# Expert weights by one 2 MB transfer per matrix, and row transposes with a step of eight

## What is computed

```python
# t: 512 tokens x 1024; each token goes to 2 of 32 experts, with a weight
def block_mlp(args):
    xb, e = args
    return (jax.nn.silu(xb @ w_gate[e]) * (xb @ w_up[e])) @ w_down[e]
# w_gate, w_up: [32, 1024, 512]; w_down: [32, 512, 1024]; all float32
```

## Time and profile before

| | |
|---|---|
| median of three runs | 2282.76 us |
| profiled execution | 2282.8 us, its span 2280.9 us |
| busy: TensorE, VectorE, ScalarE, GpSimd | 96%, 65%, 55%, 13% of the span |
| read from DRAM | 362.9 MB |
| transfers of expert weights | 192 of 1024 KB |
| mean granted TensorE clock | 0.985 |

### The profile page before, as it was taken

The page is one execution under the profiler, slowest core; times in us unless marked ns, Lnnn a source line. Parts: engine busy times, 40 slices in busy tenths (PEclk is TensorE's granted clock), DMA queues, the critical chain, the costliest instruction groups (busy, mean ns, idle before and its releaser), DMA issues. The chain is left out here.

```text
span 2280.9 us, 31925 instructions
## 1 busy us (share of the span) xinstructions
PE 2191.4 (96%) x12430; PEld 1735.7 (76%) x12430; DVE 1480.9 (65%) x1872; ACT 1250.7 (55%) x1695; POOL 300.8 (13%) x342
## 2 busy tenths in 40 slices
PE   7999999999999999899999999999995999999997
PEld 6878658877768787898888888888684777777774
DVE  3533862558888678665324573453447999988897
ACT  4324552478884454652315423244434888888885
POOL 2000001023320122640000000000011111122220
PEclk9999999999999999999999999999996999999999
DMA  6122117422224433011232213333136999999996
GB/s 239 56 74 93 37 38 247 138 75 93 93 83 157 149 112 149 22 40 56 81 104 93 93 47 121 111 122 137 56 141 245 401 405 410 403 406 399 401 398 241
DMA packets 121731, 385.61 MB, mean 169 GB/s; under 512 B 9548, under 2 KB 38532, under 8 KB 96400
## 3 DMA queue, kind: packets, MB, share of 16 engines
q1 hardware_dynamic: 106688, 333.54, 39.3%
q0 software_dynamic: 14416, 44.12, 5.7%
q10 hardware_dynamic: 512, 6.34, 0.7%
HBM read 362.89 MB, written 28.89 MB: 172 GB/s over the span
## 5 line engine op out<-in xcount | busy, mean ns | idle before, releaser
L2387 DVE TENSOR_TENSOR w_lo<-raw,w_hi 128x2048 fp32r<-128x2048 f32 x117 | 268.8, 2298 | 458.2 <-ACT w_hi L1730 458.0
L1730 ACT ACTIVATE w_hi<-raw 128x2048 fp32r<-128x2048 f32 x117 | 223.8, 1913 | 404.6 <-PE bank L900 367.3
L900 PE MATMUL bank<-hT_hi,w_hi 128*128 128x512 f32 x512 | 200.7, 392 | 4.6 <-DVE hT_lo L2451 2.3
L900 PE MATMUL bank<-hT_lo,w_hi 128*128 128x512 f32 x512 | 200.0, 391 | 0.0
L900 PE MATMUL bank<-hT_hi,w_lo 128*128 128x512 f32 x512 | 199.9, 391 | 0.0
L1111 PE MATMUL bank<-hT_hi,w_hi 128*128 128x512 f32 x432 | 173.8, 402 | 0.9 <-DVE hT_lo L2451 0.9
L1111 PE MATMUL bank<-hT_hi,w_lo 128*128 128x512 f32 x432 | 168.2, 389 | 0.0
L1111 PE MATMUL bank<-hT_lo,w_hi 128*128 128x512 f32 x432 | 168.1, 389 | 0.0
L3238 DVE TENSOR_TENSOR e_lo<-eraw,e_hi 128x2048 fp32r<-128x2048 f32 x62 | 141.8, 2288 | 35.6 <-ACT e_hi L2272 34.8
L3122 DVE TENSOR_TENSOR e_lo<-raw,e_hi 128x2048 fp32r<-128x2048 f32 x64 | 146.5, 2289 | 8.8 <-ACT e_hi L2255 8.5
L3122 DVE TENSOR_TENSOR w_lo<-raw,w_hi 128x2048 fp32r<-128x2048 f32 x64 | 144.3, 2285 | 5.8 <-ACT w_hi L2255 5.5
(11 more groups left out here) (608 smaller groups left out, 5202.3 us busy)
## 6 DMA issues: line engine op xcount, KB each, us to landing
raw<-expert_w_gate SPq DMA_DIRECT2D x64, 1024.0 KB
raw<-expert_w_up SPq DMA_DIRECT2D x64, 1024.0 KB
eraw<-expert_w_down SPq DMA_DIRECT2D x64, 1024.0 KB
raw<-w_in SPq DMA_DIRECT2D x40, 1024.0 KB
raw<-even_w_in SPq DMA_DIRECT2D x18, 1024.0 KB
raw<-odd_w_in SPq DMA_DIRECT2D x16, 1024.0 KB
raw<-even_w_out SPq DMA_DIRECT2D x8, 1024.0 KB
raw<-odd_w_out SPq DMA_DIRECT2D x8, 1024.0 KB
```

The source lines that it names most:

```text
L900: mm = pe.matmul(out, st, mv, start=first and x == 0, stop=last and x == 2)
L1730: act.activation(split_to(m)[0][:], raw[n % RAW][:], ACT.Copy).then_inc(sem("hi_done"), 1)
L2387: dve.tensor_tensor(split_to(m)[1][:], raw[split_of[m] % RAW][:], f32(split_to(m)[0][:]), ALU.subtract).then_inc(sem("lo_done"), 1)
```

## The change

The four raw buffers become one tensor `raws`, of which `raw[s]` are views at the same places. A matrix is fetched whole, into `whole[j]` (gate, up, down), by one DMA of 2 MB: partition p gets rows 8p to 8p+7 of gate or up (16 KB side by side in DRAM and in the partition), or rows 4p to 4p+3 of down as before, now both unit halves at once. Everything behind the transfer still works by units of 1 MB, as views of `whole`. The refetch of gate waits for units 0 and 1 of the expert before, that of up for units 2 and 3, that of down for both of its units. The readers of both units of a matrix wait for its one transfer. Since a partition now holds rows 8p to 8p+7, `rows_T` takes every eighth column of `xg`.

```diff
-    raw = [place(f"raw{s}", [P, 4, 512]) for s in range(RAW)]
+    raws = place("raws", [P, 4 * RAW, 512])
+    raw = [raws[:, 4 * s:4 * s + 4] for s in range(RAW)]
...
-    eraw = [raw[(len(units) + k) % RAW] for k in range(4)] + [view(f"eraw{k}", 2, [P, 4, 512], at=8192 * k) for k in range(2)]
+    assert len(units) % RAW in (0, 2)
+    whole = [raws[:, 4 * s:4 * s + KD] for s in ((len(units) + k) % RAW for k in (0, 2))] + [view("eraw_dn", 2, [P, KD, 512])[:]]
+    eraw = [w[:, 4 * u:4 * u + 4] for w in whole for u in range(2)]
...
-        def expert(e, k):
-
-            if k < 4:
-                w = io["expert_w_gate_2" if k < 2 else "expert_w_up_2"][0]
-                return w[bass.ds(e, 1)].rearrange("a (h p k) n -> p (a h) k n", p=P, k=4)[:, k % 2]
-            w = io["expert_w_down_2"][0]
-            return w[bass.ds(e, 1)].rearrange("a (p k) (h n) -> p (a k h) n", p=P, h=2)[:, 4 * (k - 4):4 * (k - 4) + 4]
-
-        def fetch(b, e, ks, first=False, d_done=0):
-            for k in ks:
+        def expert(e, j):
+
+            w = io[("expert_w_gate_2", "expert_w_up_2", "expert_w_down_2")[j]][0][bass.ds(e, 1)]
+            if j < 2:
+                return w.rearrange("a (p k) n -> p (a k) n", p=P)
+            return w.rearrange("a (p k) (h n) -> p (a k h) n", p=P, h=2)
+
+        def fetch(b, e, js, first=False, d_done=0):
+            for j in js:
                 if not first:
-                    if k < 4:
-                        sp.wait_ge(sem("gu_lo"), 4 * b + (k - 3))
+                    if j < 2:
+                        sp.wait_ge(sem("gu_lo"), 4 * b + (2 * j - 2))
                     else:
-                        sp.wait_ge(sem("d_lo"), 2 * b + (k - 5 - d_done))
-                sp.dma_start(eraw[k][:], expert(e, k)).then_inc(sem(f"e_in{k}"), 16)
-
-        GU, DN = range(4), (4, 5)
-        for k in GU:
-            u = units[len(units) - RAW + k]
-            sp.wait_ge(sem("lo_done"), u["split"] + 1)
-            fetch(0, 0, [k], True)
+                        sp.wait_ge(sem("d_lo"), 2 * b - d_done if d_done else 2 * b)
+                sp.dma_start(whole[j][:], expert(e, j)).then_inc(sem(f"e_in{2 * j}"), 16)
+
+        GU, DN = (0, 1), (2,)
+        for j in GU:
+            for u in units[len(units) - RAW + 2 * j:len(units) - RAW + 2 * j + 2]:
+                sp.wait_ge(sem("lo_done"), u["split"] + 1)
+            fetch(0, 0, [j], True)
...
             for f in range(KD):
-                rows = xg[:, 512 * (f // 4) + f % 4:512 * (f // 4) + 512:4]
+                rows = xg[:, f:D:KD]
...
-                pe.wait_ge(*after(f"e_in{4 + u}", 16 * NE))
+                pe.wait_ge(*after("e_in4", 16 * NE))
...
-                act.wait_ge(*after(f"e_in{u}", 16 * b + 16))
+                act.wait_ge(*after(f"e_in{2 * (u // 2)}", 16 * b + 16))
...
-            act.wait_ge(*after(f"e_in{4 + u}", 16 * b + 16))
+            act.wait_ge(*after("e_in4", 16 * b + 16))
```

More of the change, by code:

```diff
@@ L1703, in _ @@
                 rows_there(b)
-                pe.matmul(psum[2][:, 0:BLK], xg[:, 0:512:4], ident[0:BLK, 0:BLK], start=True, stop=True)
+                pe.matmul(psum[2][:, 0:BLK], xg[:, 0:D:KD], ident[0:BLK, 0:BLK], start=True, stop=True)
                 rows_T(b)
```

## The result

The changed kernel takes **2316.95 us** (median; 2315.3 to 2320.43), the kernel before 2282.3 on the same chip: ratio 1.0153, 95% interval 1.0141 to 1.0165. Forecast were 2287 us and a range of 2276 to 2302: wrong by 30 us, on the slower side. The profiled execution took 2315.3 us, 32.5 more than the one before.

A forecast was written before the change was run, and what follows sets the result against it. The prediction took TensorE's pace to bound the loop's first half and the DMA stream's bytes the second. From 2282.8 us, -7.0 + 4.0 + 2.8 + 2.6 + 2.0 = +4.4 gave 2287 us, range 2276 to 2302.

The forecast's parts named there:

- part 3: Expert loop: three whole buffers leave little room before refetch but no stall; 0.1 us per expert, +2.8 us.
- Part 1: Expert loop's weight transfers: half as many packets, 16 KB instead of 8, gain 0.24 us per expert, -7.0 us.
- Part 2: Start of the loop: refetches wait for both halves, +3.0 us, and the first gather is delayed, +1.0; sum +4.0.
- Rival (b): Weight transfers in the loop: the long packets gain nothing, so no -7.0; 2294 us, chance 0.16.
- Part 4: Tail: down of expert 30 lands whole and later, +2.6 us; y_dram reads come behind down of 31, +2.0.
- Part 5: Row transposes on TensorE: loading xg with a step of eight instead of four costs 0 (bound 0.6 us per expert).
- (d): Row transposes on TensorE: step of eight costs as much again as step of four; 2297 or 2312 us, chance 0.10.
- (a): Expert loop: the queue runs dry as down's refetch comes late, 0.5 us or more per expert; 2298 us, chance 0.20.

The follow-up runs named there:

- Late release and late landing: Kernel before, 1 MB transfers kept; a matrix's halves are refetched only when both are split, and readers wait for both halves: 2315.89 us, ratio 1.0139.
- The series above: Changed kernel (2316.95 us), then inside its loop VectorE's split of each second unit halved (2300.17 us), then ScalarE's halved too (2298.73 us); timing only.
- the late release alone: Kernel before, with both halves of a buffer fetched again only when both are split; readers still wait by halves: 2288.48 us, ratio 1.0019.
- two reorderings: Changed kernel with both units of down split before the product: 2338.02 us; changed kernel with y copies ahead of down's first split: 2317.53 us.

## Why the prediction was wrong

**The sum against the traces.** Up to expert 2's transposes +1.0 us was forecast (the gather) and +2.1 measured; over the loop -7.0 + 3.0 + 2.8 = -1.2 forecast and +26.9 measured; behind it +4.6 forecast and +3.4 measured.

**The step that failed is part 3, the shallower queue**: 0.1 us per expert and +2.8 us were taken, with +0.5 as the upper bound; measured, with parts 1 and 2 in it, each expert costs 26.9 / 29 = 0.93 us more. Late release and late landing alone, with the old packets, make 32 of the 34.7 us.

The inputs of this part came out: landing to refetch was forecast at 7.7 us and is 7.5, and up still has 3.1 us to run when down is issued again; less 0.3 for the issue and 1.8 for a start that leaves 1.0 us to spare, forecast 1.1. Wrong was the rule that I made of them: as long as a refetch reaches the queue before it is empty, it costs nothing, so each buffer could be judged by its slack alone. In none of the 27 turns did down's refetch meet an empty queue, and the loss came all the same. The series above shows that it goes with the splits, and so with the time to the refetch: 1.1 us less of it took 0.55 us off the period, 1.6 us less took 0.64.

Each of the three buffers runs a circle: issue to landing 9 to 10 us, landing to refetch 7 to 7.5, in sum the period of 17.0. (With one buffer per matrix this sum is the period in any case; that it comes to 17.0 explains nothing by itself.) The landing waits for the issue, the issue for ScalarE's and VectorE's splits, and these for the landing, of this buffer and of the ones ahead of it in the engines' order. With halves the circle is broken at two places: a split starts while the other half is still under way, and a fetch goes out while the other half is being split. Either one is nearly enough (+3.5, +4.5 us); without both it costs 32.

I had also reckoned a start of 1.8 us as the only price of a queue that is nearly empty. There is a second one: the packets themselves. Engine time per expert rose from 15.66 to 16.07 us here, and to 0.950 x 457 / 169.08 x 6.29 = 16.15 with 8 KB packets at the same depth (late release and late landing); it is 15.63 when the buffers come back early. Why a packet takes longer on a queue that is short, the traces don't show.

**Part 1** (-7.0) did not come: the long packets give 0.03 us per expert when the buffers come back early (between -0.08 and +0.17 by halves of the loop) and 0.08 on the short queue, 1 to 2 us in all. Rival (b) was right on this. The prices of 0.314 for 8 KB and 0.616 for 16 came from stretches of 6 and 8 us; a difference of 2% between two such rows is not a price. The Trainium skill (Perfetto Trace Analysis, "DMA Optimizations") says that batching from 2 KB into 4 or 8 KB can help much, and that splitting transfers may let some start sooner. The kernel before already stands at the 8 KB where the first ends, so no run here tests it; the second is what the change gave up, and the trace agrees with it: waiting for the whole and releasing the whole cost 32 us.

**Part 2** was two terms. The gather was forecast at +1.0 and cost 11.26 - 7.76 = 3.5 us, of which 2.1 are left at expert 2's transposes: four rows per engine, each behind one packet that is 0.31 us longer, is not what delayed it. With the large transfers held back it took 4.89 us. The late start of the stream, +3.0, lies inside the +26.9 and isn't separated by any run; in the late release alone, which starts the stream late too, the 29 periods took 468.3 us, only 1.5 more than before. Its pieces are near the forecast: gate of expert 2 went out at 1754.93 (forecast 1752.85 in the sum, "about 1754" among the signs), gate of expert 3 at 1770.69 (1767.3), and the window of the earlier trace rows has a DMA share of 0.70 instead of 0.91, 3.2 us less in 15:
```profile
1751.00:1766.00 15.00, 14.30 (x79) 11.73 (x78) 10.34 (x9) 10.33 (x10) 2.35 (x1) 1.00 0.70 246
```

**Part 4**: +4.6 forecast, +3.4 measured. The sum is near by luck, for none of its pieces came as forecast. From expert 31's row transposes to the landing of down of 30 it was 2268.39 - 2259.01 = 9.4 us, before 8.6: +0.8, where +2.6 stood. From there to the first read of y_dram it was 7.9 us instead of 10.4, since the scatter was through sooner (at most 4.2 us after its issue at 2272.17, before 6.5): -2.5, which I had not foreseen. The reads are issued at 2276.32 right behind down of 31:
```profile
2259.24 16.90 SPq L661 DMA_DIRECT2D eraw_dn<-expert_w_down  x2
2276.32 2.17 SPq L681 DMA_DIRECT2D raws<-y_dram  x4
```
Their times from issue to landing (least, median, most), before and after:
```profile
DMA to landing us min/median/max: 4.9/7.1/9.2
DMA to landing us min/median/max: 10.0/12.2/14.2
```
The first read, which VectorE waits for, takes 10.0 us instead of 4.9: +5.1 behind the last matrix, where +2.0 had been taken (0.8 - 2.5 + 5.1 = 3.4). The 7.09 us of the earlier trace rows are the second read, not the first.

**Part 5** was right in its 0: the layout and the step alone change nothing. The weight loads of the row transposes, against the earlier trace rows:
```profile
L1605 PEld LDWEIGHTS bank<-masks,xg x256: 181/201/203, 1741.9 to 2259.8; 64*128 64x128 f32 x128
```
0.201 us with the step of eight, 0.215 with four, so eight is no slower. But the step from 0.140 to 0.215, on which part 5 and (d) rest, can't be put down to the step of four: the 0.140 of the earlier trace rows is another tile at another place. Contiguous loads of 128 columns in the same loop of the kernel before took 0.188 (mean):
```profile
L1622 PEld LDWEIGHTS bank<-e_lo,bT 128*128 128x128 f32 x256 | 48.1, 188 | 9.9
```
The Trainium skill (SBUF — State Buffer, "Door 1: The DMA port swizzle") would have four fp32 free, and in the same note a penalty for each access that goes to a new 16-byte line, which is so from a step of four on. The trace agrees with neither reading in which eight costs more than four, and (d) is out; whether four costs anything over contiguous, loads of another shape (0.188) don't settle.

Of the rivals, **(a) came nearest**, with a queue that suffers from late refetches at every expert, but it didn't name what happened. It had the queue run dry from about 9 us between landing and refetch, at 0.5 us or more per expert (2298 us, chance 0.20); measured are 7.5 us, a queue that isn't empty at down's refetch, and 0.93 us. Its test, "DMA share below 0.98", could not see it, for the share is 0.99. What did answer is the rate, 385 instead of 399 GB/s, and the time from issue to landing.

What stays open is how the 17.0 us fall on the single waits: shorter work on both engines took away 0.64 of the 0.93 us (17.03 to 16.39), and two reorderings that shorten one circle gained nothing or lost. A fourth buffer, which would test the depth alone, wasn't tried.

## What to carry to other kernels

A transfer of twice the size on the same buffers halves nothing but the number of packets, and takes away two overlaps at once: the reader starts later and the buffer is free later. Before merging, take the time from landing to refetch (all work that stands between on the in-order engines) off the period; the rest is all that the next transfer has in the queue. For down it was 16.4 - 4.5 = 11.9 us for the first half, 1 MB, before, and by the forecast's own numbers 16.4 - 7.7 = 8.7 us for 2 MB after, whose bytes alone take 5.2. That the second is still longer than 5.2 + 1.8 was not enough. How much more is enough, these runs don't say in general: 6.0 instead of 7.5 us to the refetch gave back most of the loop's loss here (18.5 of 26.9 us). The cheap test is the one of the late release and late landing, which needs no new layout. And read a DMA queue's health from GB/s and from issue to landing, not from its busy share; a small gather that everything waits for goes out ahead of large loads, with the loads held back.

## What the hardware showed that was not expected

A DMA queue can be busy 0.99 of the time and 4% slower: 385 to 387 GB/s where a deep queue gives 399 to 406 (at a share of 1.01 to 1.02), with either packet size. A gather of 64 rows of 4 KB took 4.9 us with no weight transfer issued until it had landed, 7.8 with three of 1 MB issued meanwhile, and 11.3 with two of 2 MB. TensorE, idle for up to 2 us at a time in front of down in the changed kernel, was granted 0.97 of its clock over the second half instead of 1.00: after a gap of 1.32 us eight matmuls of down took 0.63 us each, at the lower of its levels (1.2 GHz; the granted clock from 2055.2 to 2058.0 us is 0.51), and then 0.39 again at 2.4 GHz:
```profile
2055.15 0.63 PE L1644 MATMUL bank<-e_hi,aT_hi 128*64 128x512 f32 x1 [1.32 <-DVE aT_lo L3256]
...
2058.83 0.39 PE L1644 MATMUL bank<-e_hi,aT_hi 128*64 128x512 f32 x1
```
